# Matmul operands that start 64 or 16 bytes further on, by stage

## The chip, the core and the metric

The kernel runs on one core of a Trainium2 chip. Its time is the device time of one execution, in microseconds (us); lower is better. The core has TensorE (PE) for matmuls, which takes a stationary operand by a weight load (PEld) and streams a moving operand against it, VectorE (DVE), ScalarE (ACT), GpSimd (POOL), and SyncE (SP), whose queue starts the DMA transfers. SBUF is the on-chip memory that the operands are read from, 128 partitions wide; PSUM takes the matmuls' results.

## What is computed

Two residual blocks, the second with two layers, over 256 tokens of width 1024, in fp32. Cut to what matters:

```python
# first block
h = rms_norm(x, norm1_w)
q, k, v, g_ret, x_lru, y_lru, gate_ret, gate_lru = split(h @ w_in)      # 1024 -> 7168
y_a = (group_norm(retention(rotary(q), rotary(k), v)) * silu(g_ret)) @ w_ret_o
y_b = (rg_lru(conv(x_lru)) * gelu(y_lru)) @ w_lru_o                     # two 256x256 block gates inside
x = x + (sigmoid(gate_ret) * y_a + sigmoid(gate_lru) * y_b) @ w_out
gate, val = split(rms_norm(x) @ ffn_w_up)                               # 1024 -> 2 x 3072
x = rms_norm(x + (gelu(conv(gate)) * val) @ ffn_w_down)
# second block, twice
x = x + 0.5 * rms_norm(swiglu(rms_norm(x)))                             # 1024 -> 2 x 2816 -> 1024
x = x + rms_norm(hybrid_mixer(rms_norm(x)))                             # w_in 1024 -> 2064 ... w_out
x = x + 0.5 * rms_norm(swiglu(rms_norm(x)))
```

## The kernel before

Every large product is made of three fp32r matmuls: an fp32 number is split into a high and a low part, and hi x hi, hi x lo and lo x hi are summed in PSUM. The activations of a stage, turned so that the model width lies over the partitions, stand in `a_hi` and `a_lo` ([128, 8, 256], 8 KB a partition each), or, for a few stages of the first block, in `b_hi` and `b_lo`. ScalarE writes the high part and VectorE the low one.

Weights come in units of 1024 x 256 numbers (1 MB). SP fills one of three `raw` buffers with two transfers, ScalarE writes `w_hi` (L612), VectorE `w_lo` (L1006), and TensorE uses the pair. Each engine's order is written out by hand as one straight program, and semaphores count units, so nothing is scheduled at run time.

The stages read their operands in one of two ways:

- 256 columns moving. `feature_major` takes a 128 x 128 block of weights as the stationary operand and streams all 256 tokens of one row of `a` or `b` against it; a unit is 48 such matmuls. So run the first projection without `v` (16 units) and the merge gates (8 units, `U1_GATES`), both on the normed input in `a`; the gates of the LRU (2 units) and `w_ret_o` (4 units) on `b`; `w_lru_o` (4 units) and the first block's up projection (24 units) on `a`; and the input projection of both mixers. There one unit a layer is turned round, `token_major`, with 256 columns of weights moving past a stationary block of `a`.
- 512 columns moving. `wide_pass` and `deep_pass` take 128 tokens of the activations as the stationary operand and stream 512 columns of weights: the `v` part of the first projection (4 units), `w_out`, the down projections (on `h_hi`, `h_lo`) and both projections of the second block's feed-forward parts.

The three matmuls of a step in `feature_major` are, stationary first, w_hi x a_hi, w_hi x a_lo, w_lo x a_hi. Each loads its stationary operand anew: the profile counts as many weight loads as matmuls.

SBUF is handed out in the order of the `sb` calls. `b_hi` and `b_lo` are given back at once, and `diag`, which the mixers use later, takes their place. As the tiles stand, every operand of an fp32r matmul begins at a multiple of 128 bytes from every other. Stages are numbered by norms: `N_UP1` is the up projection of the first block, `N_F` the final norm of the first block, which feeds the second block's first feed-forward part, and from `N_L` on three per layer: mixer, second feed-forward part, the next layer's first.

Of the kernel before, what the change touches and what calls it, by code (L numbers as in the profile page):

```python
# [125 lines left out]

(N_UP1, N_F, N_L) = (0, 1, 2)
NORMS = N_L + 3 * LAYERS


# [70 lines left out]
def build(nc, io, out):  # L201
    with ExitStack() as ctx:  # L202
        def sb(name, shape, dt=F32, scope=ctx):
            return scope.enter_context(nc.sbuf_tensor(name, shape, dt))
# [7 lines left out]
        sq = sb("sq", [P, KT, T])  # L212
        a_hi, a_lo = sb("a_hi", [P, KT, T], F32R), sb("a_lo", [P, KT, T], F32R)
        bs = ExitStack()
        b_hi, b_lo = sb("b_hi", [P, KT, T], F32R, scope=bs), sb("b_lo", [P, KT, T], F32R, scope=bs)
        bs.close()
        diag = sb("diag", [P, 32, P])
        raw = [sb(f"raw{s}", [P, KT, UC]) for s in range(NS)]
        w_hi = [sb(f"w_hi{s}", [P, KT, UC], F32R) for s in range(NS)]
# [363 lines left out]
        @block.scalar  # L583
        def _(act):
            count = {"chain": 0, "normed": 0, "y": 0, "x": 0}

# [58 lines left out]
            def turned_hi(i, t, group, col):  # L645

                for h in range(2):
                    act.wait_ge(xt_full, x_count(i, t, h))
                    for k in range(4 * h, 4 * h + 4):
                        at = k % 4 * P  # L650
                        ins = nc.scalar.activation(a_hi[:, k, t * P:t * P + P], xt_bank(t, h)[:, at:at + P], ACT.Identity,
                                                   scale=vecs[:, group, col + k:col + k + 1])
                    ins.then_inc(a_hi_ready, 1)
# [55 lines left out]
            for u in range(12, 16):  # L709
                hi(u + 2)  # L710
            operand_hi(b_hi[:, :, :], xc[:, :, :], op(1))
            act.wait_ge(psm_free, PSM_O + 1)
# [27 lines left out]
            for n in range(8):  # L740
                hi(U1_GATES + n + 2)
                g = G1_GATES + n
                act.wait_ge(unit_used, USED[U1_GATES + n])
                if n == 4:
                    act.wait_ge(ge_done, 1)
                dst = ga if n < 4 else gb
                for f in range(2):
                    k = 2 * (n % 4) + f
                    col = 16 + 8 * (n // 4) + k
                    nc.scalar.activation(dst[:, k, :], stream[g % 3][:, f * T:f * T + T], ACT.Tanh,  # L750
                                         bias=half_b[:, col:col + 1], scale=0.5).then_inc(act_gate, 1)
                if n == 0:
                    act.wait_ge(ge_cube, 1)
                    nc.scalar.activation(gel[:, :, :], gel[:, :, :], ACT.Tanh, scale=SQ2PI * GELU_C).then_inc(ge_th, 1)
                    operand_hi(b_hi[:, :, :], o_ret[:, :, :], op(2), U1_GATES)
                    act.wait_ge(lru_act, 1)
                    nc.scalar.activation(a_sq[:, :, :], a_lru[:, :, :], ACT.Square).then_inc(lru_act, 1)
                if n == 4:
                    act.wait_ge(v_ready, 1)
                    nc.scalar.activation(la, la, ACT.Sqrt).then_inc(sqrt_done, 1)  # L760
            for n in range(8):
                hi(U1_RETO + n + 2)
                if n == 0:
                    operand_hi(a_hi[:, :, :], y_lru[:, :, :], op(3), U1_RETO)
                if n >= 4:
                    m = n - 4
                    operand_hi(b_hi[:, 2 * m:2 * m + 2, :], ga[:, 2 * m:2 * m + 2, :], op(4 + m), U1_LRUO)
            hi(U1_OUT + 2)
# [84 lines left out]
            def between(i, last, scale, group=None, col=None, next_scale=None):  # L853
# [16 lines left out]
                if to_mixer:  # L870
                    hi(last + 3)

            for l in range(LAYERS):
                c0, g0 = U1_END + UL * l, G1_END + GL * l
# [109 lines left out]
        def _(dve):  # L984
# [52 lines left out]
            def turned_lo(i, t, group, col):  # L1037

                for h in range(2):
                    dve.wait_ge(a_hi_ready, KT + x_count(i, t, h))  # L1040
                    for k in range(4 * h, 4 * h + 4):
                        at, tok = k % 4 * P, slice(t * P, t * P + P)
                        V.scalar_tensor_tensor(out=a_lo[:, k, tok], in0=xt_bank(t, h)[:, at:at + P],
                                               scalar=vecs[:, group, col + k:col + k + 1],
                                               in1=a_hi[:, k, tok].bitcast(F32), op0=ALU.mult,
                                               op1=ALU.subtract).then_inc(a_split, 1)
# [167 lines left out]

            operand_lo(b_lo[:, :, :], xc[:, :, :], b_hi[:, :, :])

# [41 lines left out]
            for n in range(8):  # L1258
# [4 lines left out]
                if n == 1:  # L1263
                    operand_lo(b_lo[:, :, :], o_ret[:, :, :], b_hi[:, :, :])
                if n == 2:
# [19 lines left out]
            for n in range(4):  # L1285
                lo(U1_RETO + n + 2)
                if n == 1:
                    operand_lo(a_lo[:, :, :], y_lru[:, :, :], a_hi[:, :, :])
                g = G1_RETO + n
                dve.wait_ge(unit_used, USED[U1_RETO + n])  # L1290
                dst = ga[:, 2 * n:2 * n + 2, :]
                V.tensor_tensor(dst, dst, pair2(stream[g % 3][:, :]), ALU.mult).then_inc(group_evac, 1)
            for n in range(4):
                lo(U1_LRUO + n + 2)
                g = G1_LRUO + n
                dve.wait_ge(unit_used, USED[U1_LRUO + n])
                dst, acc = gb[:, 2 * n:2 * n + 2, :], ga[:, 2 * n:2 * n + 2, :]
                V.tensor_tensor(dst, dst, pair2(stream[g % 3][:, :]), ALU.mult).then_inc(group_evac, 1)
                dve.wait_ge(group_evac, g + 1)
                V.tensor_tensor(acc, acc, dst, ALU.add).then_inc(op_ready, 1)  # L1300
                if n:
                    operand_lo(b_lo[:, 2 * n - 2:2 * n, :], ga[:, 2 * n - 2:2 * n, :], b_hi[:, 2 * n - 2:2 * n, :])
# [139 lines left out]
            def between(i, last, at, group=None, col=None, next_eps=None):  # L1442
# [22 lines left out]
                if to_mixer:  # L1465
                    lo(last + 2)
                    lo(last + 3)

            for l in range(LAYERS):
                c0, g0 = U1_END + UL * l, G1_END + GL * l  # L1470
# [212 lines left out]
        def _(pe):  # L1683
            passed = {"n": 0}

            def mm(dst, lhs, rhs, start, stop):
# [32 lines left out]

            def token_major(s, dst, col, width, at, begin, tiles=range(TT), ready=None):  # L1720

# [69 lines left out]
            def inverse_rms(rstd):  # L1791
# [3 lines left out]
                ins.then_inc(ps7_full, 1)  # L1795

            def keep_warm(n):

                for _ in range(n):
                    mm(psm[:, 3, 0:T], a_hi[:, 0, 0:P], a_hi[:, 0, :], True, True)  # L1800

# [80 lines left out]
            for m in range(2):  # L1882
                c = U1_RG + m
                split_unit(c)
                for n in range(4):
                    g = G1_RG + 4 * m + n
                    bank_free(g)
                    ins = feature_major(c % NS, stream[g % 3], BOTH, b_hi, b_lo, True, True, kts=(2 * n, 2 * n + 1))
                    if n < 3:
                        ins.then_inc(rg_done, 1)  # L1890
                end_pass(ins, c)
# [3 lines left out]
            for n in range(4):  # L1895
                project(U1_RETO + n, G1_RETO + n, stream[(G1_RETO + n) % 3], b_hi, b_lo)
            pe.wait_ge(op_split, 3)
            for n in range(4):
                project(U1_LRUO + n, G1_LRUO + n, stream[(G1_LRUO + n) % 3], a_hi, a_lo)
            def out_ready(k):  # L1900
                pe.wait_ge(op_split, 4 + k // 2)

            for c, t in tail_passes(range(U1_OUT, U1_UP)):
                n, m = WIDE_ORDER[c - U1_OUT]
                if (c, t) == (U1_UP - 1, 1):
                    turn(N_UP1, 0, y_gain)
                wide_pass(c, t, y_bank(t, n), b_hi, b_lo, range(4 * m, 4 * m + 4), m == 0, m == 1,
                          out_ready if (n, t) == (0, 0) else None)
# [4 lines left out]
            for j in range(NF1):  # L1913
                project(U1_UP + j, G1_UP + j, stream[(G1_UP + j) % 3], a_hi, a_lo, a_ready(N_UP1, 1) if j == 0 else None)

# [27 lines left out]
            def ffn(c0, f, i, next_turn):  # L1943

                for c, t in head_passes(range(c0, c0 + NF2)):
                    j = c - c0
# [15 lines left out]
            for l in range(LAYERS):  # L1962
# [3 lines left out]
                ffn(c0, 2 * l, i, lambda: turn(i, 0, x_t))  # L1966
                cm, gm = c0 + UL_MIX, g0

                def bank(n):
# [81 lines left out]

                unit(0)
                token_major(cm % NS, bank(0), 0, UC, 0, True, (0,), a_ready(i, 0))
                turn(i, 1, x_t)
                end_pass(token_major(cm % NS, bank(0), 0, UC, 0, True, (1,), a_ready(i, 1)), cm)
                unit(1)
# [192 lines left out]
```

## Time and profile before

| what | value |
|---|---|
| time, median of 3 runs | 1464.42 us (1464.41 to 1464.76) |
| the profiled execution: its time | 1465.04 us |
| its span, first to last instruction | 1463.2 us |
| mean granted TensorE clock | 0.998 of 2.4 GHz |
| TensorE busy | 1436.5 us, 98% of the span |
| VectorE, ScalarE, GpSimd busy | 66%, 50%, 6% |
| HBM read | 256.69 MB, 176 GB/s over the span |

A matmul's record runs from the start of its work to the end of it as modelled, and the records of a steady stream overlap. So the pace of the stream is read from the distance of two starts, not from the mean length of a record. A record of fp32 type is one of two into which an fp32 matmul is divided; fp32r matmuls have one.

### The profile page before, as it was taken

What the parts mean: (1) busy time and instruction counts of PE and PEld (TensorE: products, weight loads), DVE (VectorE), ACT (ScalarE), POOL (GpSimd) and SP (SyncE); (2) the same over time, 40 slices, a digit from 0 to 9 for tenths busy, and PEclk for the clock granted to TensorE, in tenths of its full rate; (3) what the DMA queues carried; (4) which work ended last, traced back from release to release, by engine and by line L of the source; (5) the groups of instructions that cost most, each with busy time, mean ns of one, the idle gap of its engine ahead of it and who ended that gap; (6) DMA issues with size and microseconds to landing.
All of it is one profiled execution on the core that took longest, in us unless ns stands there. A gap on an engine that the chain in (4) does not pass through costs nothing. (4 is left out here: it accounts for less than half of the span.)

```text
span 1463.2 us, 21310 instructions
## 1 busy us (share of the span) xinstructions
PE 1436.5 (98%) x8888; PEld 1262.6 (86%) x8888; DVE 967.7 (66%) x1165; ACT 736.1 (50%) x936; POOL 93.6 (6%) x107
## 2 busy tenths in 40 slices
PE   7999999999999999999999999999999999999998
PEld 7899999899988788888987888878888898788886
DVE  6968786687864765646886666557565578766644
ACT  5534853555543644446565444444444466544442
POOL 0001000000000000000630000000000035000000
PEclk9999999999999999999999999999999999999999
DMA  7745465666656476455434765557754463466542
GB/s 249 234 127 189 157 192 184 173 188 174 191 184 200 155 233 216 173 189 145 145 101 136 224 188 187 180 166 230 228 189 164 149 180 102 122 209 186 188 155 104
DMA packets 251411, 259.13 MB, mean 177 GB/s; under 512 B 26659, under 2 KB 213428, under 8 KB 251316
## 3 DMA queue, kind: packets, MB, share of 16 engines
q1 hardware_dynamic: 250432, 255.49, 55.3%
q10 hardware_dynamic: 884, 2.28, 0.5%
q8 instruction: 70, 1.15, 0.3%
q14 instruction: 25, 0.20, 0.0%
HBM read 256.69 MB, written 1.05 MB: 176 GB/s over the span
## 5 line engine op out<-in xcount | busy, mean ns | idle before, releaser
L1006 DVE TENSOR_TENSOR w_lo<-raw,w_hi 128x2048 fp32r<-128x2048 f32 x240 | 547.3, 2283 | 317.0 <-ACT w_hi L612 316.7
L612 ACT ACTIVATE w_hi<-raw 128x2048 fp32r<-128x2048 f32 x240 | 456.2, 1901 | 333.4 <-PE psm L1687 152.3
L1687 PE MATMUL stream<-a_hi,w_hi 128*128 128x256 f32 x1072 | 306.5, 286 | 2.7 <-DVE a_lo L1025 1.5
L1687 PE MATMUL stream<-a_hi,w_lo 128*128 128x256 f32 x1072 | 303.9, 284 | 0.0
L1687 PE MATMUL stream<-a_lo,w_hi 128*128 128x256 f32 x1072 | 303.9, 283 | 0.0
L1687 PE MATMUL stream<-w_hi,a_hi 128*128 128x512 f32 (+1 forms) x576 | 225.4, 391 | 8.2 <-DVE w_lo L1006 5.9
L1687 PE MATMUL stream<-w_hi,a_lo 128*128 128x512 f32 (+1 forms) x576 | 221.4, 384 | 0.0
L1687 PE MATMUL stream<-w_lo,a_hi 128*128 128x512 f32 (+1 forms) x576 | 221.0, 384 | 0.0
L1687 PEld LDWEIGHTS stream<-a_hi,w_hi 128*128 128x128 f32 x1072 | 206.2, 192 | 5.0 <-issue 2.9
L1687 PEld LDWEIGHTS stream<-a_lo,w_hi 128*128 128x128 f32 x1072 | 206.3, 192 | 0.0
L1687 PEld LDWEIGHTS stream<-a_hi,w_lo 128*128 128x128 f32 x1072 | 206.2, 192 | 0.0
L1687 PE MATMUL psm<-w_hi,h_hi 128*128 128x512 f32 x448 | 175.0, 391 | 0.0
L1687 PE MATMUL psm<-w_hi,h_lo 128*128 128x512 f32 x448 | 174.4, 389 | 0.0
L1687 PE MATMUL psm<-w_lo,h_hi 128*128 128x512 f32 x448 | 174.3, 389 | 0.0
L1687 PEld LDWEIGHTS stream<-w_hi,a_hi 128*128 128x128 f32 x576 | 108.3, 188 | 31.3 <-DVE w_lo L1006 8.4
L1687 PEld LDWEIGHTS stream<-w_hi,a_lo 128*128 128x128 f32 x576 | 108.2, 188 | 22.0
L1687 PEld LDWEIGHTS stream<-w_lo,a_hi 128*128 128x128 f32 x576 | 108.4, 188 | 20.1
L1687 PEld LDWEIGHTS psm<-w_hi,h_lo 128*128 128x128 f32 x448 | 84.1, 188 | 17.7
L1687 PEld LDWEIGHTS psm<-w_hi,h_hi 128*128 128x128 f32 x448 | 84.1, 188 | 17.2
L1687 PEld LDWEIGHTS psm<-w_lo,h_hi 128*128 128x128 f32 x448 | 84.1, 188 | 17.1
L533 POOL TENSOR_TENSOR rs<-var,mhalf 128x1 f32<-128x1 f32 x28 | 15.2, 543 | 1146.2 <-DVE var L1051 1114.8
L835 ACT ACTIVATE gu<-stream,rs 128x256 f32<-128x256 f32 x68 | 32.2, 474 | 72.9 <-PE stream L1687 72.9
(290 smaller groups left out, 1718.5 us busy)
## 6 DMA issues: line engine op xcount, KB each, us to landing
raw<-in_ffn_w_up SPq DMA_DIRECT2D x136, 512.0 KB, 5.0
raw<-in_ffn_w_down SPq DMA_DIRECT2D x104, 512.0 KB, 4.4
raw<-in_ffn_w_gate SPq DMA_DIRECT2D x88, 512.0 KB, 4.0
raw<-in_w_in SPq DMA_DIRECT2D x80, 512.0 KB, 4.7
raw<-in_w_out SPq DMA_DIRECT2D x24, 512.0 KB, 4.4
raw<-in_w_ret_o SPq DMA_DIRECT2D x8, 512.0 KB, 4.1
raw<-in_w_lru_o SPq DMA_DIRECT2D x8, 512.0 KB, 4.0
diag<-in_conv_diag SPq DMA_DIRECT2D x8, 512.0 KB, 5.8
```

What stands on the lines that cost most here:

```text
L533: nc.gpsimd.tensor_tensor(to, of, mhalf[:, 0:1].broadcast_to([P, n]), ALU.pow).then_inc(rstd_ready, 1)
L612: nc.scalar.activation(w_hi[s][:, :, 0:n], raw[s][:, :, 0:n], ACT.Copy).then_inc(w_hi_ready, 1)
L835: nc.scalar.activation(th_t[:, 2 * (g % 2) + t, :], up_bank(g, t)[:, 0:UC], ACT.Tanh, scale=rs4[:, 2 + t:3 + t]).then_inc(th_ready, 1)
L1006: V.tensor_tensor(w_lo[s][:, :, 0:n], raw[s][:, :, 0:n], w_hi[s][:, :, 0:n].bitcast(F32), ALU.subtract).then_inc(w_split, 1)
L1687: return nc.tensor.matmul(dst, lhs, rhs, start=start, stop=stop, skip_group_check=True)
```

## The change

`a_hi` and `a_lo` become one tile, `a_pair`, with 128 numbers (512 bytes) to spare, and likewise `b_pair`. A stage looks up where in the joined tile its pair begins: `A_AT` and `B_AT` count in numbers of 4 bytes, so 16 is 64 bytes and 4 is 16 bytes. Writers and readers of a stage take the same views. The first projection (with the merge gates and with `v`, which read the same input) begins at 16 bytes; the LRU's gates, `w_ret_o`, `w_lru_o`, the first block's up projection and the mixers' input projections at 64 bytes; the other stages, which are the 512-column ones, at 0. `b_rest` keeps the tail of `b_pair` from being given to another tile. What is allocated behind `a_pair` and `b_pair` moves by 512 or 1024 bytes. `keep_warm`, which nothing called, is gone. Every engine has the same instructions in the same order as before.

```diff
-(N_UP1, N_F, N_L) = (0, 1, 2)
+(N_LRU, N_IN, N_UP1, N_F, N_L) = (-2, -1, 0, 1, 2)
 NORMS = N_L + 3 * LAYERS
+B_RG, B_RETO, B_OUT, B_MIX = range(4)
+A_AT = {N_IN: 4, N_LRU: 16, N_UP1: 16, N_F: 0, N_L: 16, N_L + 1: 0, N_L + 2: 0, N_L + 3: 16, N_L + 4: 0}
+B_AT = {B_RG: 16, B_RETO: 16, B_OUT: 0, B_MIX: 0}
...
-        a_hi, a_lo = sb("a_hi", [P, KT, T], F32R), sb("a_lo", [P, KT, T], F32R)
+        a_pair = sb("a_pair", [P, 2 * KT * T + 128], F32R)
         bs = ExitStack()
-        b_hi, b_lo = sb("b_hi", [P, KT, T], F32R, scope=bs), sb("b_lo", [P, KT, T], F32R, scope=bs)
+        b_pair = sb("b_pair", [P, 2 * KT * T + 128], F32R, scope=bs)
         bs.close()
         diag = sb("diag", [P, 32, P])
+        b_rest = sb("b_rest", [P, 128])
+
+        def operand_pair(space, at):
+
+            both = space[:, at:at + 2 * KT * T].rearrange("p (s k n) -> p s k n", s=2, k=KT)
+            return both[:, 0], both[:, 1]
+
+        def a_tiles(stage):
+
+            return operand_pair(a_pair, A_AT[stage])
+
+        def b_tiles(stage):
+
+            return operand_pair(b_pair, B_AT[stage])
+
+        a_hi, a_lo = a_tiles(N_IN)
...
             def turned_hi(i, t, group, col):
 
+                a_hi, _ = a_tiles(i)
...
-            operand_hi(b_hi[:, :, :], xc[:, :, :], op(1))
+            operand_hi(b_tiles(B_RG)[0], xc[:, :, :], op(1))
...
-                    operand_lo(a_lo[:, :, :], y_lru[:, :, :], a_hi[:, :, :])
+                    operand_lo(a_tiles(N_LRU)[1], y_lru[:, :, :], a_tiles(N_LRU)[0])
...
-                project(U1_RETO + n, G1_RETO + n, stream[(G1_RETO + n) % 3], b_hi, b_lo)
+                project(U1_RETO + n, G1_RETO + n, stream[(G1_RETO + n) % 3], *b_tiles(B_RETO))
...
-                project(U1_LRUO + n, G1_LRUO + n, stream[(G1_LRUO + n) % 3], a_hi, a_lo)
+                project(U1_LRUO + n, G1_LRUO + n, stream[(G1_LRUO + n) % 3], *a_tiles(N_LRU))
...
-                project(U1_UP + j, G1_UP + j, stream[(G1_UP + j) % 3], a_hi, a_lo, a_ready(N_UP1, 1) if j == 0 else None)
+                project(U1_UP + j, G1_UP + j, stream[(G1_UP + j) % 3], *a_tiles(N_UP1),
+                        a_ready(N_UP1, 1) if j == 0 else None)
...
             def ffn(c0, f, i, next_turn):
 
+                a_hi, a_lo = a_tiles(i - 1)
...
+                a_hi, a_lo = a_tiles(i)
+                b_hi, b_lo = b_tiles(B_MIX)
```

## Rows read from the trace of the kernel before

**Rows 1.** The page, engines: busy us (share of the span) and instructions of each.

```profile
PE 1436.5 (98%) x8888; PEld 1262.6 (86%) x8888; DVE 967.7 (66%) x1165; ACT 736.1 (50%) x936; POOL 93.6 (6%) x107
```

**Rows 2.** Groups, PE: out<-moving,stationary, shapes, count | busy us, mean ns | idle before.

```profile
L1687 PE MATMUL stream<-a_hi,w_hi 128*128 128x256 f32 x1072 | 306.5, 286 | 2.7 <-DVE a_lo L1025 1.5 <-DVE a_lo L1043 1.1
L1687 PE MATMUL stream<-w_hi,a_hi 128*128 128x512 f32 (+1 forms) x576 | 225.4, 391 | 8.2 <-DVE w_lo L1006 5.9 <-DVE a_lo L1043 2.4
L1687 PE MATMUL stream<-b_hi,w_hi 128*128 128x256 f32 x96 | 27.4, 285 | 1.0 <-DVE e_xl L1244 1.0
...
L1687 PE MATMUL stream<-w_hi,a_hi 128*128 128x512 f32 x544 | 216.2, 397 | 5.9 <-DVE w_lo L1006 5.9
```

**Rows 3.** Stretches (us from the start): busy us and count by engine, clock, DMA.

```profile
core 0: us, PE busy (x) PEld busy (x) DVE busy (x) ACT busy (x) POOL busy (x), PEclk, DMA share, GB/s
...
280.00:416.00 136.00, 136.00 (x1136) 136.00 (x1135) 109.86 (x159) 75.77 (x114) 0.00 (x0) 1.00 0.66 186
420.00:478.00 58.00, 58.00 (x257) 48.04 (x256) 27.76 (x21) 21.40 (x19) 0.54 (x1) 1.00 0.55 185
...
278.30:416.70 138.40, 138.22 (x1152) 138.25 (x1153) 112.13 (x167) 77.47 (x117) 0.00 (x0) 1.00 0.65 183
```

**Rows 4.** Timeline, PE: start us, length us; 256 columns at 400, 512 at 450.

```profile
399.75 0.28 PE L1687 MATMUL stream<-a_hi,w_lo 128*128 128x256 f32 x1
...
400.95 0.28 PE L1687 MATMUL stream<-a_hi,w_hi 128*128 128x256 f32 x1
...
449.68 0.39 PE L1687 MATMUL psm<-w_lo,h_hi 128*128 128x512 f32 x1
...
451.49 0.39 PE L1687 MATMUL psm<-w_hi,h_hi 128*128 128x512 f32 x1
```

**Rows 5.** Groups, weight loads: from 280 to 416 us, then from 420 to 478.

```profile
L1687 PEld LDWEIGHTS stream<-a_hi,w_hi 128*128 128x128 f32 x379 | 72.8, 192 | 0.0
...
L1687 PEld LDWEIGHTS psm<-w_hi,h_hi 128*128 128x128 f32 x86 | 16.1, 188 | 3.4
```

**Rows 6.** Early, at the lower clock: the stretch, then PE's timeline there.

```profile
18.20:20.10 1.90, 1.90 (x9) 1.88 (x9) 1.72 (x5) 1.56 (x3) 0.00 (x0) 0.50 0.84 265
...
18.23 0.42 PE L1687 MATMUL stream<-a_lo,w_hi 128*128 128x256 f32 x1
18.45 0.42 PE L1687 MATMUL stream<-a_hi,w_lo 128*128 128x256 f32 x1
18.66 0.50 PE L1687 MATMUL stream<-a_hi,w_hi 128*128 128x256 f32 x1
```

**Rows 7.** fp32 records: timeline rows of runs, and min/median/max ns by tile.

```profile
747.15 1.89 PE L1687 MATMUL ps<-up,diag 128*128 128x256 f32 x8
...
10.95 3.29 PE L1687 MATMUL stream<-keep 128*128 128x128 f32 x28
...
505.96 0.60 PE L1937 MATMUL psm<-keep,hb 128*128 128x128 f32 x4
...
L1687 PE MATMUL ps<-up,diag x42: 377/379/484, 721.4 to 753.4; 128*128 128x256 f32 x42
...
L1937 PE MATMUL psm<-keep,hb x176: 270/272/273, 506.0 to 1403.0; 128*128 128x128 f32 x176
...
L1687 PE MATMUL stream<-keep x28: 275/275/275, 10.9 to 14.0; 128*128 128x128 f32 x28
```

**Rows 8.** After an interruption: PE's timeline, and the weight loads from 131.1 to 131.45.

```profile
131.03 0.28 PE L1687 MATMUL stream<-a_lo,w_hi 128*128 128x256 f32 x1
...
131.38 0.28 PE L1687 MATMUL stream<-a_lo,w_hi 128*128 128x256 f32 x1
...
L1687 PEld LDWEIGHTS stream<-a_hi,w_lo 128*128 128x128 f32 x2 | 0.4, 188 | 0.0
L1687 PEld LDWEIGHTS stream<-a_hi,w_hi 128*128 128x128 f32 x1 | 0.2, 189 | 0.0
```

**Rows 9.** The fill queue's waits from 280 to 416 us; the first projection's stretch.

```profile
SPq L406 <- DVE w_lo L1006: 112.5, 24, 9.7
...
15.60:41.20 25.60, 25.28 (x192) 24.65 (x192) 21.66 (x37) 15.25 (x17) 0.00 (x0) 0.93 0.77 256
```

More of the change, by code:

```diff
@@ L584, in _ @@
         def _(act):
+            a_hi, _ = a_tiles(N_IN)
             count = {"chain": 0, "normed": 0, "y": 0, "x": 0}
@@ L754, in _ @@
                     nc.scalar.activation(gel[:, :, :], gel[:, :, :], ACT.Tanh, scale=SQ2PI * GELU_C).then_inc(ge_th, 1)
-                    operand_hi(b_hi[:, :, :], o_ret[:, :, :], op(2), U1_GATES)
+                    operand_hi(b_tiles(B_RETO)[0], o_ret[:, :, :], op(2), U1_GATES)
                     act.wait_ge(lru_act, 1)
@@ L763, in _ @@
                 if n == 0:
-                    operand_hi(a_hi[:, :, :], y_lru[:, :, :], op(3), U1_RETO)
+                    operand_hi(a_tiles(N_LRU)[0], y_lru[:, :, :], op(3), U1_RETO)
                 if n >= 4:
                     m = n - 4
-                    operand_hi(b_hi[:, 2 * m:2 * m + 2, :], ga[:, 2 * m:2 * m + 2, :], op(4 + m), U1_LRUO)
+                    operand_hi(b_tiles(B_OUT)[0][:, 2 * m:2 * m + 2, :], ga[:, 2 * m:2 * m + 2, :], op(4 + m), U1_LRUO)
             hi(U1_OUT + 2)
@@ L1213, in _ @@
                             ins.then_inc(op_ready, 1)
-            operand_lo(b_lo[:, :, :], xc[:, :, :], b_hi[:, :, :])
+            operand_lo(b_tiles(B_RG)[1], xc[:, :, :], b_tiles(B_RG)[0])
             def heads(tile, b):
@@ L1263, in _ @@
                 if n == 1:
-                    operand_lo(b_lo[:, :, :], o_ret[:, :, :], b_hi[:, :, :])
+                    operand_lo(b_tiles(B_RETO)[1], o_ret[:, :, :], b_tiles(B_RETO)[0])
                 if n == 2:
@@ L1300, in _ @@
                 V.tensor_tensor(acc, acc, dst, ALU.add).then_inc(op_ready, 1)
+                b_hi, b_lo = b_tiles(B_OUT)
                 if n:
@@ L1467, in between @@
                     lo(last + 3)
+            b_hi, b_lo = b_tiles(B_MIX)
             for l in range(LAYERS):
@@ L1684, in _ @@
             passed = {"n": 0}
+            a_hi, a_lo = a_tiles(N_IN)
             def mm(dst, lhs, rhs, start, stop):
@@ L1718, in _, with token_major @@
             BOTH = [(block_cols(0), 0), (block_cols(1), T)]
-            def token_major(s, dst, col, width, at, begin, tiles=range(TT), ready=None):
+            def token_major(s, dst, col, width, at, begin, a_hi, a_lo, tiles=range(TT), ready=None):
                 for t in tiles:
@@ L1795, in inverse_rms @@
                 ins.then_inc(ps7_full, 1)
-            def keep_warm(n):
-                for _ in range(n):
-                    mm(psm[:, 3, 0:T], a_hi[:, 0, 0:P], a_hi[:, 0, :], True, True)
             pe.wait_ge(ident_loaded, 16)
@@ L1887, in _ @@
                     bank_free(g)
-                    ins = feature_major(c % NS, stream[g % 3], BOTH, b_hi, b_lo, True, True, kts=(2 * n, 2 * n + 1))
+                    ins = feature_major(c % NS, stream[g % 3], BOTH, *b_tiles(B_RG), True, True, kts=(2 * n, 2 * n + 1))
                     if n < 3:
@@ L1906, in _ @@
                     turn(N_UP1, 0, y_gain)
-                wide_pass(c, t, y_bank(t, n), b_hi, b_lo, range(4 * m, 4 * m + 4), m == 0, m == 1,
+                wide_pass(c, t, y_bank(t, n), *b_tiles(B_OUT), range(4 * m, 4 * m + 4), m == 0, m == 1,
                           out_ready if (n, t) == (0, 0) else None)
@@ L1967, in _ @@
                 cm, gm = c0 + UL_MIX, g0
+                a_hi, a_lo = a_tiles(i)
+                b_hi, b_lo = b_tiles(B_MIX)
                 def bank(n):
@@ L2052, in _ @@
                 unit(0)
-                token_major(cm % NS, bank(0), 0, UC, 0, True, (0,), a_ready(i, 0))
+                token_major(cm % NS, bank(0), 0, UC, 0, True, a_hi, a_lo, (0,), a_ready(i, 0))
                 turn(i, 1, x_t)
-                end_pass(token_major(cm % NS, bank(0), 0, UC, 0, True, (1,), a_ready(i, 1)), cm)
+                end_pass(token_major(cm % NS, bank(0), 0, UC, 0, True, a_hi, a_lo, (1,), a_ready(i, 1)), cm)
                 unit(1)
```

## The prediction

> **What bounds the kernel now.** I read the page first. TensorE is busy for 1436.5 us of a span of 1463.2 us [rows 1], so whatever shortens or lengthens its steady stream moves the end almost one to one. Then I read the groups of matmuls, to see how they divide into the two kinds of stage that the change tells apart [rows 2]. In the 256-column stages the activations are the moving operand: 3 x 1072 matmuls on `a` and 3 x 96 on `b`, and to these come 3 x 32 with the weights moving, which are the difference between the 576 of the group with two forms and its 544 of 512 columns. That makes 3 x 1200 = 3600 matmuls. In all other stages the moving operand has 512 columns.
>
> A busy engine says nothing of its pace, since the records overlap, so the third view is the start times inside a long steady stretch [rows 3, 4]. From 280 to 416 us TensorE does nothing but 256-column matmuls, 1136 of them in 136.00 us, and ten steps from 399.75 to 400.95 us take 1.20 us: 120 ns each. From 420 to 478 us it does nothing but 512-column ones, and eight steps from 449.68 to 451.49 us take 1.81 us: 226 ns each. So 256 more columns cost 106 ns, and either kind pays about 13.5 ns on top of its columns. This surplus is what a shift of operands could touch: 3600 x 13.5 ns = 48.6 us, 3.3% of the time.
>
> Is the surplus a fixed cost of swapping the stationary operand? Two rows speak against that. Early on, where the granted clock was 0.50 (the lower of the two levels, 1.2 GHz), two steps take 0.43 us, from 18.23 to 18.66 us: 215 ns each, which is the 2 x 106 ns of the columns and nothing more [rows 6]. And the fp32 matmuls of the convolution taps, also 256 columns, start 0.216 us apart at the full clock, (1.89 - 0.38) / 7 [rows 7]: they load a stationary operand each too, and take their columns at half the rate. The surplus is there only where TensorE draws four bytes per partition in each cycle of the full clock while the next weights are being loaded beside it. That looks like the two reads getting in each other's way, and a collision of that sort can depend on where the two operands start.
>
> **The change part by part.** It removes, adds and moves no instruction on any engine; names and addresses alone differ. In before all operands of the fp32r matmuls start at the same place within 128 bytes. In after, 2448 of the 3600 have the activations 64 bytes further on, and the 1152 of the first projection and of the merge gates (24 units of 48) 16 bytes further on. 96 matmuls of 512 columns, those of `v`, read the same tile as the first projection, so their stationary operand moves by 16 bytes too. The writers of these tiles (the splits on ScalarE and VectorE) write as many elements as before. Everything allocated later moves by whole multiples of 512 bytes, for which I take nothing. The function that is deleted is called nowhere.
>
> What a shift does to one 256-column step is shown nowhere in this trace, since no two fp32r operands there stand differently. I bound it from both sides.
>
> - The most that can go. A step can't be shorter than its columns, 106 ns. Nor can it be shorter than its weight load: 28 warm-up records of 128 columns take 3.29 us in all, (3.29 - 0.275) / 27 = 112 ns apart, though their own columns need less, and four transposes with a load of the same size each start (0.60 - 0.27) / 3 = 0.11 us apart [rows 7]. So 8 to 11 ns a step, 29 to 40 us.
> - The nearest row to a partial gain. Within 256-column stages the weight loads take 192 ns, within 512-column ones 188 ns [rows 5]: beside the denser stream a load is held up for another 4 ns. Just after an interruption, before the two streams have settled, the same matmuls run faster for a few steps: from 131.03 to 131.38 us three steps take 0.35 us, 117 ns each, and the loads in that stretch take 188 or 189 ns [rows 8]. So 3 to 4 ns less is a state that these very matmuls take up where the two streams stand otherwise in time, and to stand otherwise in address is the nearest thing to it.
> - The other end. Nothing excludes that the new offset is a worse one. The price I put on it is the same 4 ns with the other sign.
>
> I take 4 ns, because rows 5 and 8 give it for the same matmuls, while the 8 to 11 ns come from matmuls with another stream beside the load. The sum: 3600 x 4 ns = 14.4 us. The 16-byte share of it is 1152 x 4 ns = 4.6 us, and if only the 64-byte shift works, 9.8 us remain.
>
> Does anything else then come late? In the stretch from 280 to 416 us a unit is 48 steps, 5.76 us. VectorE is busy for 109.86 of these 136 us, 4.65 us a unit, ScalarE for 75.77 us, and the queue that fills the weight buffers waits 112.5 us for the split of an old buffer to finish, so it is ahead of TensorE [rows 3, 9]. Even at 112 ns a unit would take 5.38 us, over VectorE's 4.65 us. The DMA engines' share there is 0.66, and in the first projection it reached 0.77 [rows 9]. So the gain is kept. In the mixers (816 of the 3600) TensorE waits now and then for others, which could eat at most their 816 x 4 ns = 3.3 us.
>
> The trace speaks of one execution of 1465.04 us with a span of 1463.2 us; 1465.04 - 14.4 = 1450.6 us. It lies 0.6 us above the median of the three runs, 1464.42 us, and on that footing the forecast is 1464.42 - 14.4 = **1450.0 us**.
>
> **The rivals.** *B: the collision goes altogether.* Then the weight load sets the step, 112 ns: 3600 x 8 = 28.8 us, 1435.6 us; at the transposes' 109 to 110 ns it is up to 39.6 us, 1424.8 us. For it: the surplus is wholly absent in the slower streams. Against it: the 512-column stages pay just the same 13 ns though their load has twice the time. By the Trainium skill ("TensorE: Matmul & The Clock Gate", section "Wait — 56ns, not 53.3ns?") warm matmuls start N / 2.4 GHz plus about 2.5 ns apart; for 256 columns this gives 109 ns, an estimate from that page, and 1425 us if the shift restored it. The trace disagrees as things stand, with 120 ns.
>
> *C: no change.* The two reads share something that doesn't care for the offset, and the surplus is the price of a load, whatever the addresses. For it: it is the same 13 ns with the activations moving and with the weights moving, and over all buffers and steps. The taps move on by 4 bytes each and keep their 0.216 us on average, so in fp32 at least an offset hardly shows [rows 7]. 3600 x 0 leaves 1464.4 us. This is also the side of the Trainium skill ("SBUF — State Buffer", section "SBUF: two separate sides"): within the engines only the port pair of VectorE and GpSimd contends, and TensorE waits for nobody, so an operand's address could not matter. Its rule agrees with the taps; the surplus at the full clock is not explained by it.
>
> *D: slower.* Steps of 120 ns may be the good case: with equal starts the two reads follow each other in the same order, and 64 bytes apart they meet more often. One such hold-up more, at the 4 ns of rows 5, makes 124 ns in all 3600 steps: +14.4 us, 1478.8 us. It decides as soon as the load's record grows past 192 ns instead of shrinking.
>
> **How the numbers follow.** The forecast, a partial gain around 4 ns (2 to 6): 0.35. B: 0.22. C: 0.27. D: 0.16. About 0.2%, 2.9 us or 0.8 ns a step, is what a measurement can tell from no change here. Faster: 0.35 + 0.22 = 0.57; within it 0.27; slower 0.16. The range goes from B's lower end, 1425 us, to C's upper edge, 1467 us, and leaves out D alone. Faster cases by themselves span 1425 to 1457 us.
>
> **What would show it.** In the profile of after, the stretch of the first block's up projection shows the step at once: 1152 matmuls in 138.4 us now, some 133.6 us if I am right, 129 us for B, unchanged for C, 143 us for D. The weight loads beside it should read 188 ns and not 192. The 512-column stages should keep 226 to 227 ns. If the gates' stretch, shifted by 16 bytes, stays at 120 ns while the up projection falls, the size of the shift matters. I would be wrong at the root if the 512-column stages moved as well, or if steps fell and TensorE's idle time rose by as much.

## The result, and the profile after

The changed kernel takes 1453.06 us (median of four, 1452.64 to 1459.12) against 1464.59 us (1464.41 to 1464.85) beside it: a ratio of 0.9927, interval 0.9916 to 0.9939, or 11.5 us less. The forecast was 1450.0 us. Three of the four times lie within 0.7 us, the fourth 6 us above them; the experiments come back to that.

The page's row of engines, answering [rows 1] (busy us, share of the span, instructions):

```profile
PE 1423.1 (98%) x8888; PEld 1247.8 (86%) x8888; DVE 968.7 (67%) x1165; ACT 735.9 (51%) x936; POOL 94.5 (7%) x107
```

The same instructions, 13.4 us less of TensorE's busy time, still 98% of a span that is now 1450.9 us. So the gain is in TensorE's own stream. Steady stretches show where, as in [rows 3] (busy us and count by engine, clock, DMA share, GB/s; the first is the up projection, then the first down projection, the gates, and `w_lru_o`):

```profile
core 0: us, PE busy (x) PEld busy (x) DVE busy (x) ACT busy (x) POOL busy (x), PEclk, DMA share, GB/s
278.00:404.00 126.00, 126.00 (x1114) 126.00 (x1113) 107.30 (x158) 74.58 (x113) 0.00 (x0) 1.00 0.70 198
410.00:466.00 56.00, 56.00 (x249) 46.37 (x248) 26.25 (x19) 20.04 (x17) 0.50 (x1) 1.00 0.58 191
158.00:200.00 42.00, 42.00 (x361) 41.97 (x361) 35.28 (x32) 33.10 (x30) 0.00 (x0) 1.00 0.55 176
226.00:245.00 19.00, 19.00 (x163) 19.00 (x163) 12.04 (x11) 6.51 (x7) 0.00 (x0) 1.00 0.50 174
```

The gates and `w_lru_o` in the kernel before:

```profile
160.00:202.00 42.00, 42.00 (x352) 42.00 (x352) 35.20 (x33) 31.84 (x30) 0.00 (x0) 1.00 0.56 177
228.00:247.00 19.00, 19.00 (x161) 19.00 (x160) 12.04 (x11) 6.40 (x7) 0.00 (x0) 1.00 0.48 167
```

The length divided by the count of loads (PEld) gives the step, the distance of two starts. A load that only overlaps an edge is counted too, so 1.6 go off the count in a 256-column stage (188 ns of record by 118 of step) and 0.8 in a 512-column one; a count can be off by one besides. That is 126.00 / 1111.4 = 113.4 ns in the up projection (64 bytes), 116.9 in the gates (16 bytes), 117.7 in `w_lru_o` (64 bytes), all of them 120 ns before. The down projection, whose operands were not shifted, keeps its 227 ns. Two stages with the same 64 bytes thus run at different paces. Weight loads in the up projection's stretch, as in [rows 5] (busy us, mean ns):

```profile
L1713 PEld LDWEIGHTS stream<-a_pair,w_hi 128*128 128x128 f32 x742 | 111.6, 188 | 0.0
L1713 PEld LDWEIGHTS stream<-a_pair,w_lo 128*128 128x128 f32 x371 | 69.6, 188 | 0.0
```

The 192 ns are 188 ns now. And one stretch got slower: `v`, 512 columns, whose stationary operand moved by 16 bytes with the rest of the first projection. Timelines, before and then after (start us, length us; `a_hi` and `a_lo` now share a name, so two rows merge into one "x2"):

```profile
54.62 0.39 PE L1687 MATMUL psm<-w_hi,a_lo 128*128 128x512 f32 x1
...
56.66 0.39 PE L1687 MATMUL psm<-w_hi,a_lo 128*128 128x512 f32 x1
```

```profile
54.65 0.39 PE L1713 MATMUL psm<-w_lo,a_pair 128*128 128x512 f32 x1
...
56.75 0.40 PE L1713 MATMUL psm<-w_lo,a_pair 128*128 128x512 f32 x1
```

Nine steps take 2.04 us in the one, 227 ns each, and 2.10 us in the other, 233 ns each.

From the first matmul of a stage to the first of the next, the trace gives (us; differences are taken before rounding):

| stage | 256-column steps | before | after | difference |
|---|---|---|---|---|
| first projection, four units before `v` | 192 | 25.6 | 25.8 | +0.2 |
| `v` | none | 22.4 | 22.9 | +0.6 |
| first projection, twelve units after `v` | 576 | 80.5 | 79.5 | -1.0 |
| gates | 384 | 46.1 | 44.9 | -1.2 |
| LRU gates, `w_ret_o`, `w_lru_o` | 480 | 59.1 | 58.1 | -1.0 |
| up projection | 1152 | 138.3 | 130.6 | -7.7 |
| two mixers' input projections | 816 | 168.2 | 166.2 | -1.9 |

These make -12.1 us of the 12.3 us by which the span fell. Nearly two thirds come from one stage.

### The profile page after: what moved, and what is told of

Same layout as the page of the kernel before. It is cut to its first block and busy times, and to the rows that moved or that the text cites. A ratio compares the mean times of both kernels' runs of the same rounds, so it can differ in the third digit from the quotient of the medians.

```text
span 1450.9 us, 21310 instructions
## 1 busy us (share of the span) xinstructions
PE 1423.1 (98%) x8888; PEld 1247.8 (86%) x8888; DVE 968.7 (67%) x1165; ACT 735.9 (51%) x936; POOL 94.5 (7%) x107
## 3 DMA queue, kind: packets, MB, share of 16 engines
HBM read 256.69 MB, written 1.05 MB: 178 GB/s over the span
## 5 line engine op out<-in xcount | busy, mean ns | idle before, releaser
L1713 PE MATMUL stream<-a_pair,w_hi 128*128 128x256 f32 x2144 | 378.2, 280 | 3.5 <-DVE a_pair L1047 1.9
L1713 PE MATMUL stream<-w_hi,a_pair 128*128 128x512 f32 (+1 forms) x1152 | 363.4, 388 | 8.1 <-DVE w_lo L1028 5.7
L1713 PEld LDWEIGHTS stream<-a_pair,w_hi 128*128 128x128 f32 x2144 | 325.9, 188 | 6.1 <-issue 3.3
L1713 PE MATMUL stream<-a_pair,w_lo 128*128 128x256 f32 x1072 | 298.4, 278 | 0.0
L1713 PEld LDWEIGHTS stream<-w_hi,a_pair 128*128 128x128 f32 x1152 | 214.2, 188 | 53.2 <-DVE w_lo L1028 8.3
L1713 PE MATMUL stream<-w_lo,a_pair 128*128 128x512 f32 (+1 forms) x576 | 221.0, 384 | 0.0
L1713 PEld LDWEIGHTS stream<-a_pair,w_lo 128*128 128x128 f32 x1072 | 201.8, 188 | 0.0
L1713 PEld LDWEIGHTS stream<-w_lo,a_pair 128*128 128x128 f32 x576 | 108.3, 188 | 20.1
L1713 PE MATMUL ps<-w_hi,a_pair 128*128 128x512 f32 x320 | 105.5, 391 | 0.0
L1713 PE MATMUL psm<-w_hi,b_pair 128*128 128x512 f32 x192 | 63.0, 398 | 1.1 <-DVE b_pair L1035 1.1
```

Of the source, the lines that this page charges most:

```text
L1713: return nc.tensor.matmul(dst, lhs, rhs, start=start, stop=stop, skip_group_check=True)
```

## The experiments

**Theory.** A weight load and the stream beside it disturb each other by an amount that depends on the distance between the two operands' places in SBUF. By the sizes in the `sb` calls, `a`, `b` and the weights stand multiples of 512 bytes apart in the kernel before, so the distance there is called 0; for `h_hi` and `h_lo`, which stand behind many small tiles, it is taken to be 0 too. **Rivals:** it is the moved allocations and not the offsets; or it is the moving operand's own place. A second question came from the profile: why two stages with one offset run at different paces.

**Once more, and with all offsets 0.** The first run changes nothing.

> The changed kernel once more, nothing edited. Theory 1 (a matmul step in a 256-column stage settles into one of several paces, and which one depends on how the stage is entered, alike in each execution): the first block's up projection again 113 ns a step, the gates' stretch 117, the LRU output's 118, and about 1453 us. Theory 2 (which pace a stage takes is chance): stages swap paces between this profile and the last, and single times scatter by about 6 us, which is 1152 steps x 5 ns.

The second:

```diff
-A_AT = {N_IN: 4, N_LRU: 16, N_UP1: 16, N_F: 0, N_L: 16, ...}
-B_AT = {B_RG: 16, B_RETO: 16, B_OUT: 0, B_MIX: 0}
+A_AT = {N_IN: 0, N_LRU: 0, N_UP1: 0, N_F: 0, N_L: 0, ...}
+B_AT = {B_RG: 0, B_RETO: 0, B_OUT: 0, B_MIX: 0}
```

> The joined tiles and every moved allocation stay; all offsets are 0 again. If the offsets do it: 120 ns a step in all 256-column stages, 1464.5 us. If the moved allocations behind the tiles do it: 1453 us as with the change.

Measured: 1454.05 us (1453.72 to 1458.38), ratio 0.9932 (0.9917 to 0.9946), and 1464.75 us, ratio 0.9999 (0.9989 to 1.0008). Stretches, first of the run once more (up projection, gates), then of the one with all offsets 0 (up projection):

```profile
278.00:404.00 126.00, 126.00 (x1114) 126.00 (x1114) 107.34 (x158) 74.61 (x112) 0.00 (x0) 1.00 0.69 194
158.00:200.00 42.00, 42.00 (x358) 41.97 (x357) 35.22 (x30) 33.81 (x31) 0.00 (x0) 1.00 0.54 177
```

```profile
282.00:412.00 130.00, 130.00 (x1086) 130.00 (x1085) 104.34 (x152) 71.91 (x109) 0.00 (x0) 1.00 0.66 187
```

With offset 0 the steps of the joined tiles take 130.00 / 1083.4 = 120 ns and the whole gain is gone, so neither the joined tiles nor the moved allocations do anything. Of the two theories in the first run neither holds as put: the up projection kept its 113 ns in both profiles, while the gates went from 116.9 to 42.00 / 355.4 = 118.2 ns; and again one time of four was 4 to 5 us above the others.

**Whose place counts.** A gap ahead of the weights moves them instead of the activations; `w_rest` keeps what lies behind at its place within 128 bytes.

```diff
+        w_gap = sb("w_gap", [P, 16])
         w_hi = [sb(f"w_hi{s}", [P, KT, UC], F32R) for s in range(NS)]
         w_lo = [sb(f"w_lo{s}", [P, KT, UC], F32R) for s in range(NS)]
+        w_rest = sb("w_rest", [P, 16])
```

In e3 all offsets of the activations are 0; in e4 those of all 256-column stages are 16 numbers, so that both operands stand 64 bytes further on.

> All activation offsets are 0; instead w_hi and w_lo start 64 bytes further on, in every stage. If the distance between the moving and the stationary operand counts, and a step of 64 bytes either way does the same: 113 to 118 ns in the 256-column stages, and the 512-column stages, where the distance is then 64 too, move away from 227 ns (faster or slower). If only the address of the moving operand counts: 256-column stages stay at 120 ns, and the 512-column stages, whose moving operand is the weights, change.

> Weights and the 256-column stages' activations both start 64 bytes further on (the first projection too), so their distance is 0 again there. If the distance counts: 120 ns a step in the 256-column stages. If the moving operand's own address counts: 113 to 118 ns as in the changed kernel. In the 512-column stages the activations stand at 0 and the weights at 64, as in the run before.

Measured: 1461.67 us and 1476.55 us. Stretches of e3 (up projection, first down projection, `w_lru_o`) and of e4 (up projection, first down projection):

```profile
278.00:402.00 124.00, 124.00 (x1097) 124.00 (x1096) 105.50 (x156) 73.96 (x111) 0.00 (x0) 1.00 0.71 199
410.00:466.00 56.00, 56.00 (x241) 45.12 (x240) 24.99 (x19) 20.06 (x17) 0.14 (x1) 1.00 0.56 188
223.00:241.00 18.00, 18.00 (x161) 18.00 (x161) 10.81 (x10) 6.82 (x5) 0.00 (x0) 1.00 0.59 206
```

```profile
282.00:412.00 130.00, 130.00 (x1086) 130.00 (x1084) 104.15 (x153) 73.02 (x111) 0.00 (x0) 1.00 0.67 188
420.00:478.00 58.00, 58.00 (x250) 46.71 (x250) 26.15 (x19) 20.08 (x17) 0.54 (x1) 1.00 0.56 182
```

With the weights alone moved, the up projection and `w_lru_o` both run at 113 ns; with both operands moved, the up projection is back at 130.00 / 1082.4 = 120 ns, though its moving operand stands 64 bytes from where it stood before. The distance decides. The same runs show the reverse in the 512-column stages, which now have a distance that they didn't have: the down projection takes 56.00 / 239.2 = 234 ns and 58.00 / 249.2 = 233 ns a step, not 227. The feed-forward up projections of the second block lose less (e3):

```profile
490.95 0.39 PE L1715 MATMUL ps<-w_lo,a_pair 128*128 128x512 f32 x1
...
493.01 0.39 PE L1715 MATMUL ps<-w_lo,a_pair 128*128 128x512 f32 x1
```

Nine steps take 2.06 us, 229 ns each. Both stages are 64 bytes off, but in opposite directions: in the down projection the stationary operand (`h_hi` or `h_lo`, moved by 128 bytes by the two gaps) begins 64 bytes further on than the moving one, in the feed-forward part the moving one begins further on. So with 512 columns the direction counts too. All this is why e4 is 11 us slower than before.

**How far, and what repeats.** One offset for all 256-column stages, the first projection included, the rest at 0: 64, 192, 448, 128 and 256 bytes.

```diff
-A_AT = {N_IN: 4, N_LRU: 16, N_UP1: 16, N_F: 0, N_L: 16, ...}
+A_AT = {N_IN: 16, N_LRU: 16, N_UP1: 16, N_F: 0, N_L: 16, ...}      # 48, 112, 32, 64 in the others, in B_AT too
```

> The changed kernel with 64 bytes for the first projection and the merge gates too, instead of 16. If 64 bytes is worth what it is in the other stages: the 768 steps of the projection past v and the 384 of the gates at 113 to 118 ns, v's 96 steps of 512 columns at 230 ns or more as in the down projection of the runs with shifted weights; 1449 to 1453 us. If 16 bytes is the better choice there: those steps slower than the 117 of the changed kernel and above 1454 us.

> All 256-column stages' activations, the first projection included, 192 bytes further on; the rest at 0. If places repeat every 128 bytes: as with 64 bytes, 113 in the up projection and near 118 in the output projections, about 1453 us. If they repeat every 256 bytes: 192 stands as 64 before, which the shifted weights showed with 113 ns in nearly all of these stages: about 1443 us.

> The same with 448 bytes. If places repeat every 512 bytes and no sooner: only this one stands as 64 before, 113 ns nearly everywhere, about 1443 us. If every 256 or 128 bytes: the same as with 192 bytes.

> The same with 128 bytes. If places repeat every 128 bytes: 120 ns everywhere and 1464.5 us, as with 0. If every 256 bytes or more: another pace than 120 ns in some stage.

> All 256-column stages' activations 256 bytes further on. If places repeat every 256 bytes: 120 ns and 1464.5 us as with 0. If they repeat later or not at all: less than 120 ns, as the 118.7 of 128 bytes or the 113 to 118 of 64.

Measured: 1458.69 us for 64 (1457.67 to 1459.13, ratio 0.9956, 0.9940 to 0.9973), and single times of 1450.22, 1454.14, 1461.28 and 1465.37 us for 192, 448, 128 and 256 (e6, e7, e8, e11). The up projection's stretch in these five, in that order, with `w_lru_o` as a second row for 448:

```profile
280.00:406.00 126.00, 126.00 (x1073) 126.00 (x1072) 103.36 (x151) 71.70 (x108) 0.00 (x0) 1.00 0.69 193
```

```profile
278.00:404.00 126.00, 126.00 (x1115) 126.00 (x1114) 107.35 (x158) 75.04 (x113) 0.00 (x0) 1.00 0.71 201
```

```profile
278.00:404.00 126.00, 126.00 (x1072) 126.00 (x1071) 102.72 (x151) 72.05 (x109) 0.00 (x0) 1.00 0.69 193
223.00:241.00 18.00, 18.00 (x161) 18.00 (x160) 11.15 (x10) 6.05 (x5) 0.00 (x0) 1.00 0.52 183
```

```profile
280.00:406.00 126.00, 126.00 (x1064) 126.00 (x1063) 102.44 (x151) 71.66 (x108) 0.00 (x0) 1.00 0.69 192
```

```profile
282.00:412.00 130.00, 130.00 (x1086) 130.00 (x1085) 104.07 (x152) 72.18 (x110) 0.00 (x0) 1.00 0.67 187
```

That is 117.7, 113.2, 117.8, 118.7 and 120.0 ns in the up projection, and 18.00 / 158.4 = 113.6 ns in the `w_lru_o` of the run with 448. With 256 bytes the old pace is back, and 128 differs from 0, so the place counts within 256 bytes. The distances 64 and 192 (448 is 192 once more) each have two paces, 113 and near 118, between which stages and runs differ; no offset that was tried is worse than 0 in the 256-column stages. With 64 in the first projection too, the up projection, whose offset was 64 all along, ran at 118 ns, and that alone explains most of the 5.6 us by which this run is behind the changed kernel: (117.7 - 113.4) x 1152 = 5.0 us. So the better time with 16 bytes there can't be put down to 16 bytes being the better distance for the first projection.

**What sets the pace.** In the trace of the changed kernel the pace changes inside `w_ret_o`, at an interruption of the stream (start us, length us):

```profile
206.43 0.28 PE L1713 MATMUL stream<-b_pair,w_lo 128*128 128x256 f32 x1
...
206.77 0.28 PE L1713 MATMUL stream<-b_pair,w_lo 128*128 128x256 f32 x1
206.98 0.50 PE L1713 MATMUL stream<-b_pair,w_hi 128*128 128x256 f32 x2
207.32 0.28 PE L1713 MATMUL stream<-b_pair,w_lo 128*128 128x256 f32 x1
...
208.38 0.28 PE L1713 MATMUL stream<-b_pair,w_lo 128*128 128x256 f32 x1
```

Three steps take 0.34 us before it, 113 ns each; the two around it are longer by 0.1 us each; then nine take 1.06 us, 118 ns each, with the same addresses, and so it stays to the end of `w_lru_o`. The run once more has another such place, inside the gates (16 bytes), before and after an interruption at 174 us:

```profile
172.84 0.28 PE L1713 MATMUL stream<-a_pair,w_lo 128*128 128x256 f32 x1
...
173.89 0.28 PE L1713 MATMUL stream<-a_pair,w_lo 128*128 128x256 f32 x1
...
174.34 0.28 PE L1713 MATMUL stream<-a_pair,w_lo 128*128 128x256 f32 x1
...
175.41 0.28 PE L1713 MATMUL stream<-a_pair,w_lo 128*128 128x256 f32 x1
```

Nine steps take 1.05 us before it and 1.07 us after it, 117 and 119 ns each. In the traces of all the shifted kernels the 256-column pace changes by a nanosecond or more only within some twenty steps after an interruption, or where the stream passes to operands at another distance; in between it is kept. To provoke such changes, one small matmul was put after each unit of the up projection in the kernel of e5:

```diff
+                spin(psm[:, 2, :], 1)
```

> The kernel of e5 (64 bytes in all 256-column stages), whose up projection ran at 118 ns throughout, with one small 128-column fp32 matmul after each of the 24 units of that stage: extra work of 24 x about 0.25 = 6 us. If the pace is settled anew at each interruption of the stream and then kept: units of 113 and units of 118 ns within the stage, changing only at the small matmuls. If the pace belongs to the stage, to its addresses or to what other engines do beside it: 118 ns in all 24 units.

Measured: 1458.61 us. The whole stage, and TensorE's timeline at the first small matmul:

```profile
276.10:412.00 135.90, 135.81 (x1198) 135.84 (x1199) 112.11 (x166) 77.35 (x117) 0.00 (x0) 1.00 0.66 186
```

```profile
281.37 0.39 PE L1713 MATMUL stream<-a_pair,w_hi 128*128 128x256 f32 x2
281.60 0.28 PE L1713 MATMUL stream<-a_pair,w_lo 128*128 128x256 f32 x1
281.71 0.38 PE L1713 MATMUL psm<-keep 128*128 128x128 f32 x2
281.85 0.48 PE L1713 MATMUL stream<-a_pair,w_hi 128*128 128x256 f32 x2
```

Neither expectation came true. All 24 units ran at 113 ns (in the trace they start 5.67 us apart throughout, 48 steps and 0.23 us for the small matmul), the first one too, before any small matmul, and the time equals that of e5 since the faster stage pays for the extra work. So the pace does not belong to the stage and its addresses, which are those of e5. An interruption is where the pace can change, but that each one draws anew isn't shown: these 24 changed nothing. What at the entry of a stage decides stays open.

**The distance where it helps, and none where it harms.** The weights 64 bytes further on with the 256-column stages' activations at 0, and the 512-column stages' activations moved with the weights (the two gaps of e3 stay in).

```diff
+A_AT = {N_IN: 0, N_LRU: 0, N_UP1: 0, N_F: 16, N_L: 0, N_L + 1: 16, N_L + 2: 16, N_L + 3: 0, N_L + 4: 16}
+B_AT = {B_RG: 0, B_RETO: 0, B_OUT: 16, B_MIX: 0}
-        pad = sb("pad", [P, 224])
+        pad = sb("pad", [P, 240])
```

> Weights 64 bytes further on; activations of the 256-column stages at 0 (64 behind them, as in e3), those of the 512-column stages and h_hi, h_lo at 64 too (distance 0 there), except v and the mixers' output. If only the distance counts: 256-column stages as in e3, 113 ns nearly everywhere, down and feed-forward stages back at 227 ns; e3's 1461.7 us less some 2 us for the first down projection and 2.5 us for each of four feed-forward parts: about 1449 us. If the weights' own place costs the 512-column stages something: they stay at 230 to 233 ns and the time at 1461 us.

Measured: 1458.55 us, ratio 0.9956 (0.9939 to 0.9972), 9 us over what was expected. The second block's feed-forward up projections are back at 227 ns (15 steps in 3.40 us), the first down projection is not: 56.00 / 241.2 = 232 ns.

```profile
500.01 0.39 PE L1715 MATMUL stream<-w_lo,a_pair 128*128 128x512 f32 x1
...
503.41 0.39 PE L1715 MATMUL stream<-w_lo,a_pair 128*128 128x512 f32 x1
```

```profile
410.00:466.00 56.00, 56.00 (x243) 45.40 (x242) 24.35 (x19) 20.06 (x17) 0.54 (x1) 1.00 0.57 188
```

The edit moved more than was meant: `w_gap`, `w_rest` and the wider `pad` moved `h_hi` and `h_lo` by 192 bytes, and the weights by 64, so they stood 128 apart. (In e3 and e4 the two gaps moved `h_hi` by 128, so there its distance was 64.) The last run drops `w_rest` and the wider `pad`, and weights and `h_hi` move by 64 together.

> As e10, but h_hi and h_lo stand at the same place within 256 bytes as the weights. In e10 the two gaps of 64 bytes had moved them by 128 more than meant, so that the down projections ran at a distance of 128. If the distance within 256 bytes counts: down projections back at 227 ns, e10's 1458.6 us less 1343 x 6.2 ns = 8.3 us, about 1450 us, with some 256-column stages at 113 and some at 118 ns; the whole between 1443 us (all at 113) and 1458 us (all at 118). If the weights' own place costs the down projections something: they stay at 232 to 233 ns and the time at 1458 us.

Measured: 1449.31 us (1447.86 to 1453.57), ratio 0.9896 (0.9881 to 0.9910): the fastest kernel here. Up projection and first down projection:

```profile
278.00:404.00 126.00, 126.00 (x1114) 126.00 (x1114) 107.51 (x158) 75.19 (x113) 0.00 (x0) 1.00 0.71 200
410.00:466.00 56.00, 56.00 (x249) 46.37 (x248) 25.78 (x20) 20.17 (x18) 0.54 (x1) 1.00 0.56 188
```

The down projection is at 56.00 / 247.2 = 227 ns with both operands moved, so the weights' own place costs it nothing: the distance within 256 bytes is what counts for it too.

## Why the prediction was right, point by point

- **The bound.** Right. TensorE's stream was the bound and still is; what fell from its steps came off the span, 12.1 of 12.3 us in the stages of the table. What the steps don't show, waits, stayed nearly as it was. VectorE kept its room: 107.30 us busy in 126.00.
- **The surplus is a disturbance between load and stream.** Right in that it depends on the distance of the two operands, and on no address by itself (e2, e3, e4, e12). What the prediction lacked is that the pace can also change where the stream is interrupted, with the same addresses. That it is the two reads that meet, and where, is argued and not shown.
- **The offset takes 4 ns from each of 3600 steps, 14.4 us.** This term was mis-sized, and its form was wrong. The mean came out at 12.3 / 3600 = 3.4 ns, but no steady stage takes 4 ns off: there are two paces, 120 - 113.4 = 6.6 ns less in the 1152 steps of the up projection (7.7 us by the table) and some 2 to 3 ns less in the gates and `w_lru_o`. The two rows that gave the 4 ns each showed a part: the load's 192 ns did become 188 ns, yet the load's record is not the step; and the 117 ns after an interruption [rows 8] is near the slower of the two paces. That the sum came within 3 us of the result is partly luck: the up projection gave 7.7 us where 1152 x 4 ns = 4.6 us were put down for it, and the other 2448 steps some 5 us where 9.8 us were.
- **Rival B, the load sets the step.** In the up projection the step comes near the prediction's bound: 113.4 ns beside the 112 ns of the warm-up records [rows 7]. That the load sets it is not shown: at the pace of the taps, 0.216 us for 256 fp32 columns, the 128 columns of a warm-up record take 108 ns by themselves, so those 112 ns are hardly a measure of the load. The sketch of what would show it gave 129 us for B and 133.6 us for my forecast, and the stage takes 130.6 us. Over the kernel it did not happen.
- **Rival C, no change.** Wrong. With nothing but a distance of 64 bytes, 113 or 118 ns take the place of 120. By the rule named with it, that TensorE waits for nobody (the Trainium skill, "SBUF — State Buffer", section "SBUF: two separate sides"), no operand's place could matter; these runs disagree.
- **Rival D, slower.** Wrong for the 256-column stages, where every distance tried was at least as fast as 0. Its mechanism exists in the 512-column stages: 227 ns at distance 0, 229 to 234 ns at 16, 64 and 128 bytes. I saw `v`'s 96 matmuls but put no price on them; it was 0.6 us.
- **16 bytes.** Right that it could work on its own: 116.9 and 118.2 ns on average in the gates of the two profiles.

## What to carry to other kernels

When a stream of matmuls runs at its columns plus a constant, look at the places of the two operands within 256 bytes: move one tile by 64 bytes with a gap, and read the steps stage by stage, since what helps 256 moving columns harms 512. The last run gets both, with a distance for the one and none for the other: 1449.31 us. Keep the distance, not the address, in mind, and count what a gap moves behind it. Judge such a change by the pace of each stage in a profile as well as by the time, because a stage can settle at another pace for reasons that have nothing to do with the edit.

## What the runs showed of the hardware that was not expected

- Steps of 256 columns at the full clock by distance within 256 bytes: 120 ns at 0, 117 or 119 at 16 (the gates of the run once more), 113 or 118 at 64 and at 192, 118.7 at 128, 120.0 at 256.
- Steps of 512 columns: 227 ns at 0, 233 at 16 (`v` after), 232 at 128 (e10). At 64 it goes by the direction: 233 to 234 with the stationary operand further on (down projections of e3 and e4), 229 with the moving one further on (feed-forward part of e3).
- Two paces at one distance, 4 to 5 ns apart, each kept over hundreds of steps: in the up projection that is 5.1 us of the kernel's time (130.6 against 135.8 us in e5), about what separates the odd time from the other three of the changed kernel and of its repetition. That those odd times had the slower up projection is inferred from the size, since no profile was taken of them.
